# Paired attentions: transposes one unit behind the scores and sums two units behind, in place of two and three

## The reference, cut to what matters

```python
sc = jnp.einsum('bqhd,bkhd->bhqk', qb, k).astype(jnp.float32) * scale
sc = jnp.where((key_pos[None, :] <= q_pos[:, None])[None, None], sc, NEG)
p = jax.nn.softmax(sc, axis=-1).astype(v.dtype)
return jnp.einsum('bhqk,bkhd->bqhd', p, v)
```

## Time and profile before

| | |
|---|---|
| median of 3 runs | 1763.96 us (1763.49 to 1764.81) |
| the profiled execution's own time | 1766.69 us |
| its span | 1764.6 us |
| PE busy | 1663.6 us (94%) |
| DVE busy | 862.7 us (49%) |
| ACT busy | 696.5 us (39%) |
| POOL busy | 726.1 us (41%) |
| sparse attention stage | about 1206 to 1266 us from the span's start |
| latent attention stage | about 1429 to 1491 us |

### The profile page before, as it was taken

How to read it: one execution, slowest core, us unless ns; L and a number is a source line. 1 busy time by engine, 2 the same in 40 slices (tenths; PEclk the granted TensorE clock), 3 DMA queues, 4 the chain that set the end, 5 groups by cost and what they waited for, 6 DMA issues and landing times. The chain is left out here.

```text
span 1764.6 us, 25147 instructions
## 1 busy us (share of the span) xinstructions
PE 1663.6 (94%) x10334; PEld 1267.5 (72%) x10334; DVE 862.7 (49%) x1448; ACT 696.5 (39%) x1187; POOL 726.1 (41%) x375
## 2 busy tenths in 40 slices
PE   5999998888999899999999999999998999999989
PEld 4866666885787587888888877476677466787777
DVE  5637876435932435533331166796414575324161
ACT  4335443223542533222233333435645346355440
POOL 5423334132744044555554445352236531563342
PEclk9999999997999999999999999999999899999999
DMA  5421111002523022332233333021114010442131
GB/s 173 133 66 48 60 48 51 4 4 84 155 85 96 13 85 85 104 97 94 91 93 99 102 132 113 13 64 56 38 52 126 18 60 13 132 155 83 54 102 60
DMA packets 39569, 138.53 MB, mean 79 GB/s; under 512 B 4384, under 2 KB 5664, under 8 KB 38304
## 3 DMA queue, kind: packets, MB, share of 16 engines
q1 hardware_dynamic: 39456, 136.93, 24.6%
HBM read 132.72 MB, written 4.19 MB: 78 GB/s over the span
## 5 line engine op out<-in xcount | busy, mean ns | idle before, releaser
L365 POOL TENSOR_TENSOR parts<-ring,parts 128x1024 fp32r<-128x1024 f32 (+3 forms) x251 | 572.7, 2286 | 827.5 <-ACT parts L356 826.9
L403 PE MATMUL banks<-h_hi,parts 128*128 128x512 f32 x1160 | 489.8, 422 | 19.0 <-PEq L287 9.6
L404 PE MATMUL banks<-h_lo,parts 128*128 128x512 f32 x1160 | 461.8, 398 | 0.0
L405 PE MATMUL banks<-h_hi,parts 128*128 128x512 f32 x1160 | 461.2, 398 | 0.0
L356 ACT CAST parts<-ring 128x1024 fp32r<-128x1024 f32 (+3 forms) x251 | 244.8, 979 | 176.6 <-PE banks L405 176.5
L403 PEld LDWEIGHTS banks<-h_hi,parts 128*128 128x128 f32 x1160 | 221.7, 191 | 89.0 <-issue 23.9
L404 PEld LDWEIGHTS banks<-h_lo,parts 128*128 128x128 f32 x1160 | 221.6, 191 | 54.2 <-issue 7.5
L405 PEld LDWEIGHTS banks<-h_hi,parts 128*128 128x128 f32 x1160 | 221.0, 191 | 51.9
L2872 ACT CAST ffn_act_hi<-ffn_gate 128x512 fp32r<-128x512 f32 x22 | 13.7, 622 | 167.1 <-DVE ffn_gate L2771 167.1
L2828 DVE TENSOR_TENSOR ffn_raw<-banks,ffn_root 128x512 f32<-128x512 f32 x22 | 15.2, 691 | 125.3 <-PE banks L405 125.2
L404 PE MATMUL banks<-ffn_act_lo,parts 128*128 128x512 f32 x176 | 68.5, 389 | 0.0
(11 more groups left out here) (567 smaller groups left out, 2943.1 us busy)
## 6 DMA issues: line engine op xcount, KB each, us to landing
ring<-weights SPq DMA_DIRECT2D x211, 512.0 KB, 3.5
ring<-weights SPq DMA_DIRECT2D x24, 256.0 KB, 2.6
ring<-weights SPq DMA_DIRECT2D x8, 384.0 KB, 3.3
x<-xT SPq DMA_DIRECT2D x2, 1024.0 KB, 6.4
x<-xT SPq DMA_DIRECT2D x1, 2048.0 KB, 7.9
x_spill<-x SPq DMA_DIRECT2D x2, 1024.0 KB, 4.8
x<-x_spill SPq DMA_DIRECT2D x1, 2048.0 KB, 8.1
outT<-x SPq DMA_DIRECT2D x8, 256.0 KB, 2.0
```

The source lines that it names most:

```text
L365: self.nc.gpsimd.tensor_tensor(self.parts[:, t % PARTS, 1, 0:w], self.ring[:, t % SLOTS, 0:w], self.parts[:, t % PARTS, 0, 0:w].bitcast(F3 ...
L403: nc.tensor.matmul(out, w.hi, x.hi, start=first, stop=False)
L404: nc.tensor.matmul(out, w.hi, x.lo, start=False, stop=False)
L405: return nc.tensor.matmul(out, w.lo, x.hi, start=False, stop=last)
```

## The change

The two distances in `attend_pairs` are smaller by one unit. Nothing else differs; `STEPS`, the banks and the buffers stay.

```diff
     NS, NB, STEPS = 6, 3, 2
-    TURN, SUM, OUT = 2, 3, 5
+    TURN, SUM, OUT = 1, 2, 5
```

## The result

The changed kernel takes 1801.93 us (median of 4, 1797.43 to 1802.50) against 1763.93 us (4 runs) for the kernel before: ratio 1.0203, 95% interval 1.019 to 1.0215. Measured again beside other kernels it took 1798.97 us (4 runs), ratio 1.0194 (1.0181 to 1.0207). It is slower, by 35 to 38 us where 30.5 were forecast. The profiled execution of the changed kernel has a span of 1800.3 us, 35.7 more than before.

A forecast was written before the change was run, and what follows sets the result against it. PE's list was taken to set the length of both paired-attention stages; added waits for DVE, net of the tail, of 14.6 us (sparse) and 15.9 us (latent), together 30.5 us, gave 1794.5 us, range 1784 to 1804 us.

The forecast's parts named there:

- What bounds the stage: Both paired attentions: PE's list sets the length, PE busy 56.68 of 60 and 59.07 of 63 us; idle PE is lost time.
- DVE's unchanged order decides: DVE's loop: line 2489 for unit j's new scores comes first, only then scaling of unit j - 1, which PE now wants.
- The waits E + 0.06 - F - H: From DVE's start: E to scaling's end, F to PE free; 0.06 restart, H first head's transposes; sparse waits 0.85 to 1.60 us.
- F of the t = 0 units: Units scoring 128 keys: time from DVE's start until PE is free, 0.68 us, kept for the latent stage; wait 0.85 us.
- the first wait: Iteration 1, DVE's first scaling beside POOL: 3.0 us, net 2.4 us after iteration 2's old 0.56; latent taken from sparse.
- the 0.18 us: Latent stage: PE free 0.18 us sooner after DVE's start, added to seven waits of t = 2 and 3.
- its 4.3 us for four latent units: Sign to look for: four units take about 4.3 us more in the latent stage, 3.7 in the sparse one.
- The sums as cover for t = 1: Units j = 5, 9, 13: sums ahead of the transposes take about 2.3 us of PE, so no wait is added.
- The tail: Stage end, DVE's start on unit 15 to last sums: 5.39 us instead of 5.69, 0.3 us less.
- The clock: Rival: idle PE lowers the clock in both stages, 10 us on top, about 1805 us; 7%.
- POOL again: Rival: POOL's other three instructions in a stage hold up scalings PE waits for, 12 us, about 1806 us; 7%.
- The other rivals: Waits partly hidden: 11 us less, 1783 us, 5%. Not slower, pipeline drains sooner: some 1763 us, 3%.

The follow-up runs named there:

- scale_first: Changed kernel with DVE's two blocks swapped, scaling of unit j - 1 before line 2489 of unit j: 1761.52 us, ratio to the kernel before 0.9979.
- turn_alone: Changed kernel with the sums put back to three units behind (TURN 1, SUM 3): 1800.3 us, ratio to the kernel before 1.0197.
- pool_waits: Changed kernel with POOL waiting in each stage until DVE has scaled the first unit: 1787.74 us, ratio 1.0125; a second time 1788.47 us, ratio 1.0139.
- before_pool_waits: Kernel before (old distances) with POOL waiting in each stage for DVE's first scaling: 1760.95 us, ratio 0.9984; a second time 1760.73 us, ratio 0.9987.
- one_wait: Kernel before with one more PE wait in iteration 1 of each stage, until DVE has scaled the first unit: 1771.69 us, ratio 1.005.
- both_steps_first: Changed kernel with both background steps of an iteration between the scores and the transposes: 1782.4 us, ratio to the kernel before 1.0089.
- null_before: Kernel before, unchanged, measured against itself: 1765.61 us, ratio 1.0009.
- changed_again: Changed kernel, unchanged, measured a second time: 1798.97 us, ratio to the kernel before 1.0194.

## Why the prediction was right, and where it was short

- **What bounds the stage.** Right. PE's list sets the length, and what PE waits is added to it: in the sparse stage the weight loads' idleness for DVE rose by 17.1 us and the stage by 16.4, of which some 15 are waiting and 1.4 clock, as reckoned below.
- **DVE's unchanged order decides.** Right, and shown by its opposite: with DVE's two blocks swapped, the same distances cost nothing (scale_first).
- **The waits E + 0.06 - F - H.** Right in the sparse stage: 1.62 us for 512 keys against 1.60. With POOL held back and the clock full that stage is 13.0 us longer than before; with the 2.0 us that POOL adds this gives 15.0, forecast 14.6. In the latent stage POOL adds 1.8 us, and it gives 15.3 + 1.8 = 17.1 us, forecast 15.9. Two terms were taken from the sparse stage and were off there. One is F of the t = 0 units, which was too large, so that their waits came out too small: an iteration of 128 keys takes 3.71 us where it took 2.51, of which 0.2 are the two more transposes, so 1.0 us of waiting in place of 0.85, 0.5 us in three units. The other is the first wait, net of what the kernel before waited in iteration 2. With POOL's wait that iteration of the kernel before fell from 3.26 to 2.65 us in the sparse stage and from 3.24 to 2.92 in the latent one, so 0.3 us less is taken off there. The remaining 0.4 us are small differences in the first wait and the others. The prediction is not quite one with itself here: its sum leaves the three t = 0 units out of the 0.18 us, its 4.3 us for four latent units counts them in, and 4.25 was measured.
- **The sums as cover for t = 1.** Right: PE goes from the sums to the transposes without a wait there, and turn_alone trades that cover for another.
- **The tail.** It came out right to the hundredth, which for a sum of five readings is in part luck. From DVE's start on unit 15 to the last sums, answering to the earlier trace rows:

```profile
1275.30 0.75 DVE L2489 CUSTOM_DVE_ANT_0 scores<-banks,a_chosen,a_q_scale 128x512 f32<-128x512 f32 x1 [2.30 <-PE banks L2449]
...
1280.69 2.37 PE L2460 MATMUL banks<-probT,a_v 128*64 128x512 f32 x16 [0.73 <-ACT probT L2527]
```

1280.69 - 1275.30 = 5.39 us, as forecast, against 5.69 before.

- **The clock.** This is the term that was mis-sized: the sum had nothing for it, and it measured about 5 us. The prediction had named a clock under 1.00 in the two stages as a sign of being wrong, and in the changed kernel that sign came (0.98 and 0.94); on this point it was wrong. In iterations 1 and 2 of the sparse stage the first profile is 0.7 us each over full clock, and in iterations 1 to 3 of the latent stage 0.7, 2.1 and 0.7 (iteration 2 takes 6.71 us where it takes 4.62 at full clock in pool_waits, iteration 3 takes 6.20 where 5.54). It was a rival with 7%, priced at 10 us, and argued away with the earlier trace rows, where a tail with waits of 0.5 to 0.9 us kept its clock. That row bore on the many short waits, for which it was right. For the wait of 2.5 us without a break in iteration 1 the stretch from 612 us in the same rows was the nearer one: in it PE had waited 2.82 us at a stretch. The rule of the Trainium skill in "TensorE: Matmul & The Clock Gate", section "A second HAM failure mode: psum-queue depth-cycling", on frequent brief idleness did not come true at these waits: 24 of the weight loads in a stage, of PE itself up to 1.4 us at a time, left the clock at 1.00 in both runs of pool_waits.
- **POOL again.** Didn't happen; of DVE's scalings in a stage only the first takes longer (2.29 and 2.10 us). The other rivals fell too: no wait was partly hidden, and the stage behind the latent one is as long as before within 0.2 us. The stretch between the two is 2.5 us shorter, but so it is in before_pool_waits with the old distances; it is the clock shown above.

Together: 15.0 + 17.1 us of waiting, 4.9 of clock, 1.2 less outside the stages: 35.8, where the span grew by 35.7. The forecast of 30.5 us had 32.1 us of waiting and tail too low by 1.6 and the clock at nothing.

## What to carry to other kernels

When a software pipeline's distance is shortened on the consumer's engine, look at where the producer's step stands in its own list: behind the newest unit's work it can't be early, whatever the distance says, and the cost is its chain less the cover, for every unit. Swap the producer's order together with the distance, or leave both: here the swap took the cost of the shorter distance away, but no run shows that the two together make the stages shorter than they were. Put a single long wait in a stretch of dense products on the bill twice, once for itself and once for the clock behind it.

## What the runs showed of the hardware that was not expected

- One idle stretch of PE of 1.8 to 2.9 us in iteration 1 was followed by products 0.43 us apart instead of 0.23 (1.2 GHz in place of 2.4), for some 4 to 11 us: in both stages of the changed kernel's first profile and in the latent stage of its second, in both stages of turn_alone and of one_wait, and behind 1.81 us in the sparse stage of both_steps_first. PE's waits of 0.4 to 1.4 us, 12 to a stage, were not (pool_waits, both times). Each of these stages begins with a pause of 1.8 or 2.3 us at its barrier, some 6 us ahead of the wait. Whether the wait alone would do it there no run separates.
- The same program's clock can fall at a place in one execution and not in another: at the start of the sparse stage, behind the 1.8 us gap at the barrier, in null_before and changed_again, and not in the first profiles of the same two programs. In null_before it was worth 0.9 us, and behind the two pauses between the stages 2.6 us. In 35 runs of the kernel before that were measured together, the mean clock goes from 0.981 in the fastest (1758.54 us) to 0.974 in the slowest (1768.56), so most of that spread of 10 us goes with the clock.
- DVE's scaling in place (128x128) took 2.29 us beside a POOL instruction and 0.28 without, ending 0.08 us after POOL's; line 2489 (256 keys), which reads a bank and a mask, took 0.48 us in either case.
